# Merging the last column group of the up projections: two matmuls for three per weight tile

## The chip, the cores and the metric

The kernel runs on one core of a Trainium2 chip. The metric is the device time of one execution in microseconds (us), as the median of several runs. TensorE is called PE here, VectorE DVE, ScalarE ACT, GpSimd POOL; L1979 is line 1979 of the kernel file.

## The reference

Two blocks of two layers each work on x with 256 tokens and 1024 features, in float32. Six feed-forward networks (FFNs) lie on the path, one after the other: two in the first block, four in the second. In short:

```python
def conv_ffn(h, w_up, conv_w, conv_b, w_down):        # FFN 0 and 1
    gu = h @ w_up                                     # 1024 -> 2 * 2816
    g, u = gu[..., :D_FF], gu[..., D_FF:]
    g = causal_depthwise_conv3(g, conv_w) + conv_b
    return (silu(g) * u) @ w_down                     # 2816 -> 1024

def swiglu(x, w13, w2):                               # FFN 2 to 5
    gate, up = jnp.split(x @ w13, 2, axis=-1)
    return (silu(gate) * up) @ w2
```

Between them stand a state-space mixer, a stick-breaking attention and, twice, a mixer of sliding-window attention and a gated delta rule. The change touches only the up projections `h @ w_up` and `x @ w13`.

## The kernel before

**Precision.** Each operand of a projection is split into a rounded part (hi) and its rest (lo), both in a rounded float32 format, and a product is made of three matmuls: hi*hi, hi*lo and lo*hi. Weights come from memory in panels of 512 rows by 512 columns (`plan`). A panel lands in `raw` (a ring of RAW = 2 slots), ACT rounds it into `w_hi` (L744, in `split_hi`), and DVE subtracts to get `w_lo` (L1239, in `split_lo`); `w_hi` and `w_lo` have SPL = 3 slots. PE waits for `lo_ready` before a panel, and frees the slot with `panel_used`. SP issues the load of panel p once `w_lo` of panel p - 2 is made.

**The up projection.** It has 11 column groups j = 0 to 10. Each group has 256 gate columns and 256 up columns, in four tiles of 128, and two panels (k tiles 0 to 3 and 4 to 7). There are two ways to compute a group:

- `features` (L1983): for each column tile and k tile the three matmuls of `product` (L1979 to L1981), each 256 tokens wide, with the sums of a group in one accumulator `acc` (1024 columns, four tiles of 256).
- `merged` (L2132): the activation's hi and rest lie side by side in `xT`, so one matmul 512 wide (L2148) multiplies `w_hi` with both and a second one 256 wide (L2149) adds `w_lo` times hi. The sums take twice the room, two accumulators of 1024 columns: half 0 for the two gate tiles, half 1 for the two up tiles.

Groups in `MERGED` (1 to 9) take the second way, groups 0 and 10 the first. Group 0 is worked through in the order in which its input arrives (L1995, L2002).

**Accumulators.** There are two, `acc[0]` and `acc[1]`, handed out in turn by a running number u (`up_uses`, L377, and `uses`): use u takes `acc[u % 2]`, and `claim(u)` (L1970) makes PE wait until use u - 2 is freed. A merged group with an even j takes two uses, u and u + 1; a merged group with an odd j takes none and lies in the two `turn_banks` (named trp in the rows). A plain group takes one use. The down projection that follows (`tokens`, L2029) takes two uses, one for each half of its 1024 columns: it has 6 panels for each half, 24 matmuls of 512 columns in a full one.

**Folding a merged group.** The hi and lo sums have to be added. In `ffn` of ACT, L783 copies the lo sums of half 0 and then of half 1 into `folds`. In `ffn` of DVE, L1375 adds half 0 (the gate), L1377 adds half 1 (the up part). For an even j, half 1 is freed by L1377 itself, half 0 by an increment of DVE's sequencer behind it, once L1375 is done. Then follow, for FFN 0 and 1, the convolution's bias tap on ACT (L790) and its two other taps on DVE (L1390, L1391), silu (L794, or L796 for FFN 2 to 5), the product with the up part (L1394), rounding into `hT_hi` (L803) and its rest `hT_lo` (L1404). A plain group goes straight from `acc` into L790 or L796.

**Order on ACT and DVE.** It is written out by `gemm`: for group j, the split of panel p0 + 3 (p0 is the first of the group's two panels), then the evacuation of group j (fold, taps, product), then the split of panel p0 + 4, then `hidden` (L803 or L1404). So for group 10 the split ahead of its evacuation is that of the second panel of the down projection. Both engines work their instructions off in this order.

The down projection waits for `hT_lo` of each pair of k tiles (`hlo_ready`); its last panel needs that of group 10.

Of the kernel before, what the change touches and what calls it, by code (L numbers as in the profile page):

```python
# [49 lines left out]
RAW, SPL = 2, 3  # L50
TRP = 4

MERGED = range(1, 10)

TWO_PI = 2 * math.pi
MAGIC = 1.5 * 2 ** 23
# [127 lines left out]
def build(nc, T, out):  # L184
# [4 lines left out]
    with es:  # L189
# [5 lines left out]
        def sem(name):  # L195
            if name not in sems:
                sems[name] = es.enter_context(nc.semaphore(name))
            return sems[name]
# [178 lines left out]
        def up_uses(name):  # L377
# [3 lines left out]
            for j, ps in enumerate(gemms[name]):  # L381
                pairs_at[name, j] = None if j in MERGED and j % 2 else n_use
                if pairs_at[name, j] is None:
                    turns.append((name, j))
                    continue
                for _ in range(2 if j in MERGED else 1):
                    filled[n_use] = (panel_used, ps[-1] + 1)
# [131 lines left out]
        def up_tiles(f, j):  # L519

            if j in MERGED:
                v = folds[:, j % 2]
            else:
                v = A4(place(f"up{f}", j))
            return v[:, 0:2], v[:, 2:4]

        def folded_no(f, j):
            return f * len(MERGED) + j - MERGED.start + 1

# [193 lines left out]
        def _(act):  # L723
# [50 lines left out]
            def ffn(f):  # L774
                def gate(j, u):
# [3 lines left out]
                    h, (g, _) = hbuf[:, hn % 2], up_tiles(f, j)  # L779
                    if j in MERGED:  # L780
                        act.wait_ge(panel_used, gemms[f"up{f}"][j][-1] + 1)
# [16 lines left out]
                def hidden(j, u):  # L798
                    if j in MERGED:
                        act.wait_ge(sem("fold_gated"), folded_no(f, j))  # L800
                    else:
                        wait_evacuated(act, u)
                    A(hT_hi[:, 2 * j:2 * j + 2, :], hbuf[:, (f * 11 + j) % 2], ACT.Copy).then_inc(sem("hhi_ready"), 1)  # L803
# [1915 lines left out]
```

## Time and profile before

| | |
|---|---|
| Time, median of 3 runs | 2141.79 us (2140.05 to 2143.49) |
| Profiled execution, its own time | 2142.33 us |
| Its span | 2140.5 us |
| PE busy with matmuls | 2075.5 us, 97% |
| PE weight loads | 1802.6 us, 84% |
| DVE, ACT, POOL busy | 1436.9 us (67%), 1060.7 us (50%), 159.5 us (7%) |
| Matmuls | 14848, each with one weight load |

The span is the time from the first to the last instruction; 1.8 us of the execution's time lie around it. A matmul's own duration is modelled and overlaps the next one's, so the pace of PE is read from the starts of its matmuls.

### The profile page before, as it was taken

How to read it: one execution, taken by the hardware profiler on the slowest of the kernel's cores; microseconds unless marked ns; L12 is line 12 of the kernel's file. 1: busy time of each engine (PE TensorE's matmuls, PEld its weight loads, DVE VectorE, ACT ScalarE, POOL GpSimd, SP SyncE). 2: the span in 40 equal slices, each digit the busy share in tenths (PEclk: the TensorE clock that was granted, in tenths of full speed). 3: DMA queues.
4: the chain of work that ended last, by engine and by line, in shares of the span. 5: the costliest groups of instructions: out<-in, count | busy, mean ns of one | idle time of the engine just before them, and what ended most of it. 6: DMA issues, size and time to landing. Idle time of an engine off the chain costs nothing.

```text
span 2140.5 us, 34287 instructions
## 1 busy us (share of the span) xinstructions
PE 2075.5 (97%) x14848; PEld 1802.6 (84%) x14848; DVE 1436.9 (67%) x1658; ACT 1060.7 (50%) x1266; POOL 159.5 (7%) x119
## 2 busy tenths in 40 slices
PE   7799999999999999999999999999999999999998
PEld 6788888988888888898778888888889977788886
DVE  8966765567765664775766776476558576677654
ACT  5545554655643553455544455345434564444542
POOL 1000000000001000440000010020005200002000
PEclk9799999999999999999999999999999999999999
DMA  7245655435555665554312475556546633135653
GB/s 153 71 156 163 197 187 167 158 118 177 178 188 186 197 197 177 176 198 138 120 41 100 154 216 182 184 184 204 186 154 203 203 119 118 42 118 171 203 187 128
DMA packets 259789, 342.45 MB, mean 160 GB/s; under 512 B 23383, under 2 KB 169469, under 8 KB 259639
## 3 DMA queue, kind: packets, MB, share of 16 engines
q1 hardware_dynamic: 254272, 329.95, 48.0%
q0 software_dynamic: 2768, 9.08, 1.4%
q10 hardware_dynamic: 2599, 1.23, 0.5%
q8 instruction: 117, 1.92, 0.4%
q14 instruction: 33, 0.27, 0.0%
HBM read 338.14 MB, written 2.10 MB: 159 GB/s over the span
## 4 chain that ended last, share of the span: by engine, by line
PE 85%; DVE 9%; DMA 1%; ACT 1%; issue 1%; POOL 0%; DVEq 0%; ACTq 0%
PE acc L1979 11%; PE acc L1981 11%; PE acc L1980 11%; PE trp L2148 10%; PE acc L2148 8%; PE trp L2149 5%; PE acc L2149 4%; PE acc L1995 3%; PE trp L1979 2%; PE trp L1981 2%; PE trp L1980 2%; DVE w_lo L1239 2%; PE acc L2002 1%; PE acc L2044 1%; DMA raw<-in_w_in 1%; PE acc L2561 1%
## 5 line engine op out<-in xcount | busy, mean ns | idle before, releaser
L1239 DVE TENSOR_TENSOR w_lo<-raw,w_hi 128x2048 fp32r<-128x2048 f32 x314 | 721.5, 2301 | 414.9 <-ACT w_hi L744 413.4
L744 ACT ACTIVATE w_hi<-raw 128x2048 fp32r<-128x2048 f32 x314 | 590.0, 1879 | 542.7 <-PE acc L1981 206.2
L2148 PE MATMUL trp<-xT,w_hi 128*128 128x512 f32 x960 | 338.5, 396 | 0.0
L2148 PE MATMUL acc<-xT,w_hi 128*128 128x512 f32 x768 | 270.8, 396 | 0.0
L2149 PE MATMUL trp<-xT,w_lo 128*128 128x256 f32 x960 | 269.4, 281 | 0.0
L2148 PEld LDWEIGHTS trp<-xT,w_hi 128*128 128x128 f32 x960 | 180.1, 188 | 43.0
L2149 PE MATMUL acc<-xT,w_lo 128*128 128x256 f32 x768 | 215.5, 281 | 0.0
L1981 PE MATMUL acc<-w_hi,hT_lo 128*128 128x512 f32 x528 | 209.3, 396 | 0.0
L1979 PE MATMUL acc<-w_hi,hT_hi 128*128 128x512 f32 x528 | 209.3, 396 | 0.0
L1980 PE MATMUL acc<-w_lo,hT_hi 128*128 128x512 f32 x528 | 209.3, 396 | 0.0
L1979 PE MATMUL acc<-xT,w_hi 128*128 128x256 f32 x704 | 201.3, 286 | 6.1 <-DVE w_lo L1239 6.1
L1980 PE MATMUL acc<-xT,w_hi 128*128 128x256 f32 x704 | 200.6, 285 | 0.0
L1981 PE MATMUL acc<-xT,w_lo 128*128 128x256 f32 x704 | 200.6, 285 | 0.0
L2149 PEld LDWEIGHTS trp<-xT,w_lo 128*128 128x128 f32 x960 | 181.4, 189 | 0.0
L2148 PEld LDWEIGHTS acc<-xT,w_hi 128*128 128x128 f32 x768 | 144.1, 188 | 34.6
L2149 PEld LDWEIGHTS acc<-xT,w_lo 128*128 128x128 f32 x768 | 145.1, 189 | 0.0
L1979 PEld LDWEIGHTS acc<-xT,w_hi 128*128 128x128 f32 x704 | 136.4, 194 | 7.4 <-issue 7.1
L1980 PEld LDWEIGHTS acc<-xT,w_hi 128*128 128x128 f32 x704 | 136.5, 194 | 0.1
L1981 PEld LDWEIGHTS acc<-xT,w_lo 128*128 128x128 f32 x704 | 136.5, 194 | 0.0
L1981 PEld LDWEIGHTS acc<-w_hi,hT_lo 128*128 128x128 f32 x528 | 99.5, 188 | 24.2
L1980 PEld LDWEIGHTS acc<-w_lo,hT_hi 128*128 128x128 f32 x528 | 99.5, 188 | 24.0
L1979 PEld LDWEIGHTS acc<-w_hi,hT_hi 128*128 128x128 f32 x528 | 99.5, 188 | 24.0
(438 smaller groups left out, 3438.7 us busy)
## 6 DMA issues: line engine op xcount, KB each, us to landing
raw<-in_ffn_w SPq DMA_DIRECT2D x184, 512.0 KB
raw<-in_w_in SPq DMA_DIRECT2D x60, 1024.0 KB
raw<-in_ffn_w_up SPq DMA_DIRECT2D x88, 512.0 KB
raw<-in_ffn_w SPq DMA_DIRECT2D x40, 1024.0 KB
raw<-in_ffn_w_down SPq DMA_DIRECT2D x20, 1024.0 KB
raw<-in_ssm_w_glu SPq DMA_DIRECT2D x16, 512.0 KB
raw<-in_kv_w SPq DMA_DIRECT2D x8, 1024.0 KB
raw<-in_w_branch_a SPq DMA_DIRECT2D x8, 1024.0 KB
```

The source lines that it names most:

```text
L744: A(w_hi[:, p % SPL, 0:kt, :], raw[:, p % RAW, 0:kt, :], ACT.Copy).then_inc(hi_ready, 1)
L1239: V_.tensor_tensor(w_lo[:, p % SPL, 0:kt, :], raw[:, p % RAW, 0:kt, :], w_hi[:, p % SPL, 0:kt, :].bitcast(F32), ALU.subtract).then_inc(lo_ ...
L1979: mm(out, ah, bh, start=first, stop=False, skip_group_check=True)
L1980: mm(out, ah, bl, start=False, stop=False, skip_group_check=True)
L1981: return mm(out, al, bh, start=False, stop=last, skip_group_check=True)
L1995: mm(out[:, n], w[:, p % SPL, k, n * P:n * P + P], src[0][:, k0 + k, :], start=i == k == 0 and w is w_hi and n % 2 == 0, stop=False, skip_ ...
L2002: ins = mm(out[:, n], w_hi[:, p % SPL, kk, n * P:n * P + P], src[1][:, k0 + kk, :], start=False, stop=i == len(gemms[name][j]) - 1 and kk ...
L2044: mm(out[:, t], src[0][:, k0 + k, t * P:t * P + P], w[:, p % SPL, k, :], start=i == k == 0 and w is w_hi, stop=False, skip_group_check=True)
L2148: mm(tile, w_hi[:, p % SPL, k, c], xT[:, k0 + k], start=i == k == 0, stop=False, skip_group_check=True)
L2149: ins = mm(tile[:, 0], w_lo[:, p % SPL, k, c], xT_hi[:, k0 + k, :], start=False, stop=i == len(gemms[name][j]) - 1 and k == kt - 1, skip_g ...
L2561: ins = mm(a[:, h * P:h * P + P], left[:, h, :], right[:, h, :], start=n == 0, stop=n == len(terms) - 1, skip_group_check=True)
```

## The change

Group 10 too is merged, in all six FFNs: its two panels are worked through with L2148 and L2149 in place of L1979 to L1981, and it goes through the folds. As it is even, it takes two accumulator uses where it took one, so all later uses have a number that is higher by one for each FFN passed. `folded_no` counts ten merged groups for each FFN where it counted nine.

```diff
-MERGED = range(1, 10)
+MERGED = range(1, 11)
```

## Rows read from the trace of the kernel before

**Rows 1.** The page: busy time of the engines; the chain that ended last, by engine.
```profile
PE 2075.5 (97%) x14848; PEld 1802.6 (84%) x14848; DVE 1436.9 (67%) x1658; ACT 1060.7 (50%) x1266; POOL 159.5 (7%) x119
...
PE 85%; DVE 9%; DMA 1%; ACT 1%; issue 1%; POOL 0%; DVEq 0%; ACTq 0%
```

**Rows 2.** Waits of PE: who waited for whom: us in total, times, longest us.
```profile
PE trp L2287 <- DVEq L1573: 6.2, 1, 6.2
PE acc L1979 <- DVE w_lo L1239: 6.1, 4, 2.3
```

**Rows 3.** Timeline of PE, FFN 0 and 1: start us, duration, engine, line, operation.
```profile
282.04 0.35 PE L1979 MATMUL acc<-xT,w_hi 128*128 128x256 f32 x1
...
293.63 0.39 PE L1979 MATMUL acc<-w_hi,hT_hi 128*128 128x512 f32 x1
...
607.63 0.39 PE L1979 MATMUL acc<-w_hi,hT_hi 128*128 128x512 f32 x1
```

**Rows 4.** Timeline of PE, FFN 2 and 4: first matmuls of group 9, group 10, down.
```profile
776.06 0.40 PE L2148 MATMUL trp<-xT,w_hi 128*128 128x512 f32 x1
...
787.37 0.28 PE L1979 MATMUL acc<-xT,w_hi 128*128 128x256 f32 x1
...
798.89 0.39 PE L1979 MATMUL acc<-w_hi,hT_hi 128*128 128x512 f32 x1
...
1508.28 0.39 PE L2148 MATMUL trp<-xT,w_hi 128*128 128x512 f32 x1
...
1519.37 0.28 PE L1979 MATMUL acc<-xT,w_hi 128*128 128x256 f32 x1
...
1530.88 0.39 PE L1979 MATMUL acc<-w_hi,hT_hi 128*128 128x512 f32 x1
```

**Rows 5.** Timelines of ACT and of DVE, FFN 2: the folds of group 9.
```profile
787.63 1.09 ACT L783 ACTIVATE folds<-trp 128x512 f32<-128x512 f32 x2 [3.73 <-PE trp L2149]
...
788.26 0.69 DVE L1375 TENSOR_TENSOR folds<-folds,trp 128x512 f32<-128x512 f32 x1 [2.03 <-ACT folds L783]
```

**Rows 6.** Timeline of DVE, FFN 0 and 1: what stands ahead of group 10's evacuation.
```profile
293.75 2.28 DVE L1239 TENSOR_TENSOR w_lo<-raw,w_hi 128x2048 fp32r<-128x2048 f32 x1
295.95 0.47 DVE L1390 SCALAR_TENSOR_TENSOR hbuf<-acc,cols,hbuf 128x255 f32<-128x255 f32 x1
...
300.36 2.29 DVE L1239 TENSOR_TENSOR w_lo<-raw,w_hi 128x2048 fp32r<-128x2048 f32 x1 [1.12 <-ACT w_hi L744]
...
607.13 2.29 DVE L1239 TENSOR_TENSOR w_lo<-raw,w_hi 128x2048 fp32r<-128x2048 f32 x1
609.34 0.48 DVE L1390 SCALAR_TENSOR_TENSOR hbuf<-acc,cols,hbuf 128x255 f32<-128x255 f32 x1
```

**Rows 7.** Timelines of DVE and of PE, near 22 us: one hand-over.
```profile
20.51 2.23 DVE L1239 TENSOR_TENSOR w_lo<-raw,w_hi 128x2048 fp32r<-128x2048 f32 x1
...
22.79 0.39 PE L1995 MATMUL acc<-xT,w_hi 128*128 128x256 f32 x1 [1.09 <-DVE w_lo L1239]
```

**Rows 8.** Timeline of PE: the longest waits behind 124 us, in brackets the idle us.
```profile
903.42 0.36 PE L1979 MATMUL acc<-xT,w_hi 128*128 128x256 f32 x1 [2.27 <-DVE w_lo L1239]
...
1095.05 0.27 PE L2566 MATMUL acc<-cst,U 64*64 64x64 f32 x1 [1.39 <-DVE U L1837]
...
1635.14 0.39 PE L1979 MATMUL acc<-xT,w_hi 128*128 128x256 f32 x1 [1.91 <-DVE w_lo L1239]
```

**Rows 9.** Windows: us, engines' busy time (instructions), PEclk, DMA share, GB/s.
```profile
905.00:910.00 5.00, 5.00 (x31) 5.00 (x31) 4.93 (x11) 1.44 (x2) 2.32 (x2) 0.67 0.97 363
910.00:915.00 5.00, 5.00 (x44) 5.00 (x43) 4.82 (x5) 3.29 (x3) 3.18 (x2) 1.00 0.34 84
...
1635.00:1640.00 5.00, 4.86 (x28) 4.89 (x29) 4.59 (x7) 1.79 (x5) 3.96 (x3) 0.66 0.75 243
...
1098.00:1103.00 5.00, 5.00 (x78) 4.14 (x77) 1.77 (x2) 4.97 (x4) 0.00 (x0) 1.00 0.00 0
```

**Rows 10.** Timeline of PE: third and sixth panel of the down projection, FFN 0.
```profile
304.88 0.40 PE L1979 MATMUL acc<-w_hi,hT_hi 128*128 128x512 f32 x1
...
321.74 0.40 PE L1979 MATMUL acc<-w_hi,hT_hi 128*128 128x512 f32 x1
```

**Rows 11.** Timeline of PE: two matmuls, 33 apart, in the v projection.
```profile
413.32 0.39 PE L1980 MATMUL acc<-w_lo,xT 128*128 128x512 f32 x1
...
420.80 0.39 PE L1980 MATMUL acc<-w_lo,xT 128*128 128x512 f32 x1
```

## The prediction

> **What bounds the kernel now.** I read the page's busy shares and the chain first, then PE's waits, then the timelines of PE, DVE and ACT around the end of an up projection. The reader is to see three things. PE is busy 97% of the span and holds 85% of the chain [rows 1]: what shortens or holds up its stream moves the end nearly one for one. Its waits are few and none of them lies at an up projection's end: the largest groups are 6.2 us at 101 us, and four waits for w_lo, 6.1 us together [rows 2]. And at an end the down projection's first matmul follows at the pace of the stream, 293.63 in FFN 0 and 798.89 in FFN 2 [rows 3, 4]: the accumulator that it claims has been free for long, because it is half 1 of group 8, folded while group 9 ran.
>
> **What the change removes: a third of group 10's weight loads.** Plain, group 10 takes 293.63 - 282.04 = 11.59 us in FFN 0, 798.89 - 787.37 = 11.52 in FFN 2 and 1530.88 - 1519.37 = 11.51 in FFN 4 [rows 3, 4]. That is 96 matmuls at 0.120. A merged group has 32 pairs. Group 9 in FFN 2 takes 787.37 - 776.06 = 11.31 us, 0.353 for a pair; in FFN 4 it takes 1519.37 - 1508.28 = 11.09, 0.347 for a pair [rows 4]. So the gain is small, 0.2 us in FFN 0 to 3, whose merged groups run nearly all at the first pace, and 0.4 in FFN 4 and 5 at the second: the columns that stream, 768 for each weight tile, are the same in both ways. If nothing else changed, the sum would be 4 x 0.2 + 2 x 0.4 = 1.6 us less.
>
> The Trainium skill, TensorE: Matmul & The Clock Gate, section "Wait — 56ns, not 53.3ns?", has a matmul cost its columns and some 2.5 ns more at full clock. By that, an estimate, one matmul fewer in each of 32 triples saves 0.08 us in a group and 0.5 us in all six. The trace speaks for more: a triple takes 360 ns and a pair 353 or 347. The stream's sum would be 0.5 less by the page and 1.6 less by the rows; the total below would rise by 1.1.
>
> **What it adds: PE waits for the fold at every up projection's end.** Group 10 now takes uses u and u + 1, and the first half of the down projection takes u + 2, which is the accumulator of group 10's half 0. Its claim waits until use u is freed, and that happens only when L783 has copied the lo sums and L1375 has added them. Behind the claim stands everything that PE has: 132 matmuls of that half, and then the rest of the program. No other claim is hit: group 10 claims what group 8 held, which was folded during group 9, and the down projection's second half claims group 10's half 1 some 30 us later. The change of parity everywhere behind leaves the order of claims as it is.
>
> The length of the wait, FFN 2 to 5. Here DVE is idle when the fold comes. Group 9 shows the chain: PE's next slot is at 787.37, ACT copies from 787.63, and L1375 runs from 788.26 to 788.95 [rows 4, 5]. That is 1.58 us behind the slot. Then DVE's sequencer sees its own semaphore, increments another, and PE starts. One such hand-over took 22.79 - (20.51 + 2.23) = 0.05 us [rows 7]; the trace shows none by way of a sequencer, so its bounds are 0.05 and twice to four times this, and I take two, 0.1. The down projection starts 1.68 us behind the slot. The split of panel p0 + 3 is ready before: it needs only group 10's first panel done. Against today, with the gain set off: in FFN 2 and 3 the slot is at 787.37 + 11.31 = 798.68, the start at 800.36 and not 798.89, +1.47 each. In FFN 4 and 5 the slot is at 1519.37 + 11.09 = 1530.46, the start at 1532.14 and not 1530.88, +1.26 each. Four of them make 2 x 1.47 + 2 x 1.26 = 5.5.
>
> FFN 0 and 1. Here DVE is late, since the taps of group 9 delay it: ahead of group 10's evacuation stands the w_lo split, from 293.75 to 296.03, and the next instruction starts at 295.95 [rows 6]. The fold add stands at that place, whatever PE does, and ACT's copies (from some 293.6, 0.55 each) are done by then. It takes 0.69 as in [rows 5], so half 0 is folded at 296.64 and PE starts at 296.74, not at 293.63: +3.1. In FFN 1 the same place is at 609.34 [rows 6], which gives 610.13 against 607.63: +2.5. In these two the group's own gain is swallowed by the wait. Together 5.6.
>
> **What it adds on ACT and DVE.** Two copies (1.09), two adds (1.37) for each FFN. They delay the split of the third down panel: today 300.36 to 302.65 in FFN 0 [rows 6], then about 2 us later, by 304.7. PE needs it at 304.88 today [rows 10] and, having waited, at 308.0. It is covered; if the wait were not there, 0.2 us would be all that is left of that cover. hT_lo of group 10 is due before the sixth panel, at 321.74 + 3.1, some 20 us after it is made. Nothing for either.
>
> **The clock.** The two longest waits behind 124 us idled PE 2.27 and 1.91 us. Right behind them the mean clock of five us is 0.67 and 0.66, and PE starts about 31 matmuls where it starts 44 at full clock [rows 8, 9]: 13 x 0.12 = 1.5 us are lost as part of the stretch runs at 1.2 in place of 2.4 GHz. Behind a wait of 1.39 us the clock stayed at 1.00 [rows 8, 9]. The new waits in FFN 0 and 1 idle PE for some 3.4 and 2.7 us, beyond both rows that fell, so I take 1.5 us for each: 3.0. Those in FFN 2 to 5 idle it for 1.7, between the row that held and the one that fell; I take nothing, and the bound is 4 x 1.5 = 6.0.
>
> **The sum.** 5.5 + 5.6 + 3.0 = 14.1 us more than the profiled execution's 2142.33, so 2156.4. The runs' median is 0.5 below that execution: 2155.9, say 2156.
>
> **The rivals.** (a) *The clock falls at all six ends.* For it: 1.7 is nearer to 1.91 than to 1.39. Against: a wait and a fall have only two cases in the trace. 2156 + 6 = 2162. (b) *The clock does not fall.* 2156 - 3 = 2153. (c) *The wait is hidden*: the first down matmuls find their accumulator free, as today, and what is left is the lighter stream. It needs half 0 freed within a matmul of group 10's end; if the fold took no longer than the 0.2 to 0.4 us that a group gains, it would break even. For it speaks that no group before this one was ever seen to wait. Against: the fold of [rows 5], with both engines idle before it, takes 1.58 us, and group 10 has no group behind it that lies elsewhere. 2141.8 - 1.6 = 2140, not slower. (d) *PE's pace changes behind the new waits.* Streams of 512 columns have two paces: 72 matmuls of the down projection take 321.74 - 304.88 = 16.86, 0.234 each, while in the v projection it is (420.80 - 413.32) / 33 = 0.227 [rows 10, 11]. If the wait put all six down projections (264 matmuls each) on the faster pace, 6 x 264 x 0.0074 = 11.7 us come back: 2156 - 11.7 = 2144. Against it: the down projection runs at 0.234 in all six FFNs, whichever pace its merged groups had, so it looks like a property of its operands. The smaller case, merged groups changing between 11.31 and 11.09 in one FFN, is worth 2 us either way.
>
> **How the numbers follow.** Forecast (clock down at FFN 0 and 1, here and there once more or less) 0.62, (a) 0.12, (b) 0.13, (c) 0.04, (d) 0.05, and 0.04 for something not seen. The time is that of the likeliest, 2156. The range reaches from (b) with the merged groups' faster pace in two FFNs, 2149, to (a) and a little more, 2163; it leaves out (c), (d) and the tail. A measurement of this kernel can tell about 0.2%, 4.3 us, from no change: slower than 2146.1 is 0.90, from (d) 0.05 and (c) 0.03 within it 0.08, faster 0.02.
>
> **What would show it.** PE's waits should list the first down matmul six times, behind DVE's fold (L1375, or the sequencer behind it), 1.6 to 1.8 us in FFN 2 to 5 and 2.5 to 3.4 in FFN 0 and 1, some 13 us together. The stretches after those in FFN 0 and 1 should have a clock below 1.00 for a part of 5 us. Group 10 should take 11.3 or 11.1 us, and PE's instruction count fall by 192, to 14656. The forecast is wrong if the down projection starts within 0.5 us of group 10's end, if the clock stays up behind 3 us, or if another stretch gives the time back: the four waits for w_lo of [rows 2] come 60 us and more behind an up projection's end, and their loads are issued relative to PE's own progress, so I expect none of it there.

## The result, and the profile after

| | before | after |
|---|---|---|
| Median of 6 runs each | 2139.2 us (2134.1 to 2143.5) | 2149.8 us (2148.4 to 2152.4) |
| Ratio to before | | 1.0056, 95% interval 1.0046 to 1.0066 |
| Profiled execution, its time; span | 2142.33; 2140.5 us | 2149.43; 2147.5 us |
| PE busy | 2075.5 us | 2070.1 us |
| Matmuls | 14848 | 14656 |

The change makes the kernel slower by 0.56%, 12.0 us (9.8 to 14.1). The ratio is not the quotient of the two medians, which are 10.6 us apart; both lie inside the interval. PE's matmuls fell by 192, as they should, its busy time by 5.4 us, and yet the end came later. The page after, first line of its busy times and the chain by engine, against [rows 1]:

```profile
PE 2070.1 (96%) x14656; PEld 1784.4 (83%) x14656; DVE 1447.3 (67%) x1670; ACT 1067.9 (50%) x1278; POOL 151.8 (7%) x119
...
PE 74%; DVE 16%; ACT 4%; DMA 2%; issue 2%; POOL 0%; DVEq 0%; SPq 0%; ACTq 0%
```

PE's share of the chain fell from 85% to 74%, and DVE's rose from 9% to 16%. The six new waits alone don't do that: a kernel further down ("fold first") has all six, and its page still says PE 85% and DVE 9%. The shift comes from FFN 0 and 1. There the fold came late because DVE was late, and from that point the chain leads back through DVE and ACT along nearly the whole up projection: `w_hi`, `w_lo`, `hT_lo`, `w_lo`, fold, taps, silu and the next `w_hi`. In FFN 2 to 5 it leaves PE only for the fold at the end. One turn of that loop in FFN 0 takes 11.35 us, here from one w_lo split of DVE to the next, where a merged group takes PE 11.31:

```profile
278.60 2.29 DVE L1239 TENSOR_TENSOR w_lo<-raw,w_hi 128x2048 fp32r<-128x2048 f32 x1 [1.11 <-ACT w_hi L744]
...
289.95 2.29 DVE L1239 TENSOR_TENSOR w_lo<-raw,w_hi 128x2048 fp32r<-128x2048 f32 x1 [1.11 <-ACT w_hi L744]
```

So in FFN 0 and 1 these two engines together are as near to being the limit as PE. PE's waits after (who waited for whom: us in total, times, longest us), against [rows 2], name the new one:

```profile
PE acc L1979 <- DVEq L1384: 10.9, 6, 2.9
...
PE acc L1979 <- DVE w_lo L1239: 4.0, 4, 1.4
```

L1384 is the increment by DVE's sequencer that frees the first half of group 10's accumulators. PE never waited for it before; now it does, once in each FFN. PE's timeline after, at the end of the up projection in FFN 0, 1 and 2 (start us, duration, and in brackets the idle us and who ended it), against [rows 3] and [rows 4]:

```profile
292.60 0.28 PE L2149 MATMUL acc<-xT,w_lo 128*128 128x256 f32 x1
295.76 0.79 PE L1979 MATMUL acc<-w_hi,hT_hi 128*128 128x512 f32 x1 [2.87 <-DVEq L1384]
...
610.98 0.28 PE L2149 MATMUL acc<-xT,w_lo 128*128 128x256 f32 x1
613.17 0.50 PE L1979 MATMUL acc<-w_hi,hT_hi 128*128 128x512 f32 x1 [1.91 <-DVEq L1384]
...
804.21 0.28 PE L2149 MATMUL acc<-xT,w_lo 128*128 128x256 f32 x1
806.01 0.51 PE L1979 MATMUL acc<-w_hi,hT_hi 128*128 128x512 f32 x1 [1.52 <-DVEq L1384]
```

The two other engines' timelines after, ACT and then DVE, show what the waits are made of. In FFN 2 both were idle: PE's last matmul starts at 804.21, ACT copies from 804.59, DVE adds from 805.22 to 805.91, and PE starts 0.10 later. In FFN 0 ACT's copies start at 292.98, but DVE is in w_lo until 295.04, and the add starts at 294.96:

```profile
292.98 1.08 ACT L783 ACTIVATE folds<-acc 128x512 f32<-128x512 f32 x2 [0.73 <-PE acc L2149]
...
804.59 1.09 ACT L783 ACTIVATE folds<-acc 128x512 f32<-128x512 f32 x2 [3.74 <-PE acc L2149]
```
```profile
292.76 2.28 DVE L1239 TENSOR_TENSOR w_lo<-raw,w_hi 128x2048 fp32r<-128x2048 f32 x1
294.96 0.68 DVE L1375 TENSOR_TENSOR folds<-folds,acc 128x512 f32<-128x512 f32 x1
...
805.22 0.69 DVE L1375 TENSOR_TENSOR folds<-folds,acc 128x512 f32<-128x512 f32 x1 [2.05 <-ACT folds L783]
```

**By stage.** From PE's starts, for each FFN the time from the first matmul of group 1 to the first of the down projection ("up"), and from there to the down projection's last ("down"):

| FFN | up before | up after | down before | down after |
|---|---|---|---|---|
| 0 | 113.42 | 116.11 | 61.61 | 63.16 |
| 1 | 113.28 | 115.14 | 61.61 | 61.72 |
| 2 | 113.28 | 114.76 | 61.61 | 61.72 |
| 3 | 113.27 | 112.72 | 61.61 | 61.72 |
| 4 | 111.47 | 114.76 | 61.61 | 61.73 |
| 5 | 111.46 | 114.76 | 61.61 | 61.72 |

FFN 1 and 2 ran their merged groups at the same pace in both profiles and show the change alone: +1.86 and +1.48. (FFN 0 did so but for its last two groups before, 11.32 and 11.35.) FFN 3, 4 and 5 also changed between the two paces of a merged group, 11.3 and 11.1 us, which nine or ten groups make 2 us. The down projection is 0.11 longer everywhere, as its first matmul behind a wait takes 0.11 more to the next, and 1.55 longer in FFN 0, where the clock fell.

### The profile page after: what moved, and what is told of

Read it like the earlier page. It is cut to its first block, busy times and chain, and to the rows that moved or that the text cites. A ratio compares the mean times of both kernels' runs of the same rounds, so it can differ in the third digit from the quotient of the medians.

```text
span 2147.5 us, 33939 instructions
## 1 busy us (share of the span) xinstructions
PE 2070.1 (96%) x14656; PEld 1784.4 (83%) x14656; DVE 1447.3 (67%) x1670; ACT 1067.9 (50%) x1278; POOL 151.8 (7%) x119
## 4 chain that ended last, share of the span: by engine, by line
PE 74%; DVE 16%; ACT 4%; DMA 2%; issue 2%; POOL 0%; DVEq 0%; SPq 0%; ACTq 0%
PE acc L1979 10%; PE acc L1981 10%; PE acc L1980 10%; PE trp L2148 7%; PE acc L2148 7%; DVE w_lo L1239 6%; PE trp L2149 4%; PE acc L2149 4%; PE acc L1995 3%; PE trp L1979 2%; ACT w_hi L744 2%; PE trp L1981 2%; PE trp L1980 2%; PE acc L2044 1%; DMA raw<-in_w_in 1%
## 5 line engine op out<-in xcount | busy, mean ns | idle before, releaser
L2148 PE MATMUL trp<-xT,w_hi 128*128 128x512 f32 x960 | 339.7, 398 | 0.0
L2148 PE MATMUL acc<-xT,w_hi 128*128 128x512 f32 x960 | 339.5, 398 | 0.0
L2149 PE MATMUL trp<-xT,w_lo 128*128 128x256 f32 x960 | 269.1, 280 | 0.0
L2149 PE MATMUL acc<-xT,w_lo 128*128 128x256 f32 x960 | 269.0, 280 | 0.0
L1979 PE MATMUL acc<-w_hi,hT_hi 128*128 128x512 f32 x528 | 210.7, 399 | 10.9 <-DVEq L1384 10.9
L2148 PEld LDWEIGHTS acc<-xT,w_hi 128*128 128x128 f32 x960 | 180.3, 188 | 44.5
L2148 PEld LDWEIGHTS trp<-xT,w_hi 128*128 128x128 f32 x960 | 180.4, 188 | 44.2
L1981 PE MATMUL acc<-w_hi,hT_lo 128*128 128x512 f32 x528 | 209.8, 397 | 0.0
L2149 PEld LDWEIGHTS trp<-xT,w_lo 128*128 128x128 f32 x960 | 181.2, 189 | 0.0
L2149 PEld LDWEIGHTS acc<-xT,w_lo 128*128 128x128 f32 x960 | 181.1, 189 | 0.0
L1979 PE MATMUL acc<-xT,w_hi 128*128 128x256 f32 x512 | 145.6, 284 | 4.0 <-DVE w_lo L1239 4.0
L1980 PE MATMUL acc<-xT,w_hi 128*128 128x256 f32 x512 | 144.9, 283 | 0.0
L1981 PE MATMUL acc<-xT,w_lo 128*128 128x256 f32 x512 | 144.9, 283 | 0.0
L1979 PEld LDWEIGHTS acc<-w_hi,hT_hi 128*128 128x128 f32 x528 | 99.8, 189 | 36.9 <-DVEq L1384 12.8
L1981 PEld LDWEIGHTS acc<-w_hi,hT_lo 128*128 128x128 f32 x528 | 99.8, 189 | 24.4
L658 POOL TENSOR_TENSOR nrm<-nrm 128x1 f32<-128x1 f32 x22 | 13.6, 617 | 1390.1 <-DVE nrm L1274 832.1
L1979 PE MATMUL trp<-w_hi,xT 128*128 128x512 f32 x256 | 104.7, 409 | 0.0
L1979 PEld LDWEIGHTS acc<-xT,w_hi 128*128 128x128 f32 x512 | 98.2, 192 | 4.7 <-issue 4.7
```

The costliest lines, as they stand in the source:

```text
L658: tt(nrm[:, 3, one], nrm[:, 0, one], nrm[:, 1, one], ALU.pow).then_inc(sem("root_ready"), 1)
L1979: mm(out, ah, bh, start=first, stop=False, skip_group_check=True)
L1980: mm(out, ah, bl, start=False, stop=False, skip_group_check=True)
L1981: return mm(out, al, bh, start=False, stop=last, skip_group_check=True)
L2148: mm(tile, w_hi[:, p % SPL, k, c], xT[:, k0 + k], start=i == k == 0, stop=False, skip_group_check=True)
L2149: ins = mm(tile[:, 0], w_lo[:, p % SPL, k, c], xT_hi[:, k0 + k, :], start=False, stop=i == len(gemms[name][j]) - 1 and k == kt - 1, skip_g ...
```

## The experiments

The table has all runs; each ratio is to the kernel before, run on the same chip in the same rounds. Differences in us below are worked out from the ratios.

| Kernel | Median us | Before, same rounds | Ratio, 95% interval |
|---|---|---|---|
| group 10 merged, down in turn bank | 2137.95 | 2138.95 | 0.9997 (0.9988 to 1.0006) |
| group 10 plain, wait added | 2159.3 | 2138.95 | 1.0092 (1.0079 to 1.0106) |
| merged, fold first | 2150.02 | 2138.95 | 1.0045 (1.0032 to 1.0057) |
| the changed kernel again | 2151.75 | 2138.95 | 1.0057 (1.0043 to 1.0071) |
| group 10 plain, down in turn bank | 2136.55 | 2136.36 | 1.0000 (0.9991 to 1.0010) |
| merged, down in turn bank, again | 2137.41 | 2136.36 | 1.0003 (0.9992 to 1.0013) |
| the kernel before, again, one execution | 2141.55 | 2136.36 | |

**The merge without the wait.** The first half of the down projection gets the turn bank that group 9 left. It takes one accumulator use less for each FFN, so its second half claims group 10's half 0 and later uses have lower numbers; nothing else of the changed kernel differs. The main lines of the edit; `...` stands for lines left out, which call `down_uses` and give this use a semaphore of its own for being freed:

```diff
+        def down_uses(f):
...
+            name = f"down{f}"
+            pairs_at[name, 0], pairs_at[name, 1] = -1 - f, n_use
...
         def A2(u):
+            if u < 0:
+                return turn_banks[0][:, :].rearrange("p (t n) -> p t n", t=2)
...
             def claim(u):
 
+                if u < 0:
+                    pe.wait_ge(sem("turn_freed"), turns.index((f"up{-1 - u}", 9)) + 1)
+                    return
```

> Group 10 is merged as in the changed kernel, but the first half of the down projection sums in turn bank 0, which group 9 left a whole group earlier, so its claim waits for nothing new. If the wait for the fold of group 10 is the cost (my theory): the six waits (10.9 us) and the clock's fall behind FFN 0 (1.5 us) go, and the time is 12 us below the changed kernel and within 2 us of the kernel before (some 2138). If the merged matmuls or the added folds themselves cost (rival): it stays within 4 us of the changed kernel, 2146 to 2154.

The ratio is 0.9997, and the whole loss is gone: 12.8 us between this kernel's ratio and that of the changed kernel in the same rounds (0.0060 x 2139). The rival, that the merged matmuls or the folds themselves cost, falls: this kernel has both. In PE's timeline of this kernel the down projection (L1998 here) follows the last merged matmul of FFN 2 at the stream's own pace, 0.12 behind it, and the line of the waits for DVE's sequencer is gone:

```profile
797.45 0.28 PE L2168 MATMUL acc<-xT,w_lo 128*128 128x256 f32 x1
797.57 0.40 PE L1998 MATMUL trp<-w_hi,hT_hi 128*128 128x512 f32 x1
```

From group 1 to the down projection FFN 1 to 5 take 113.07 us each, where the kernel before took 113.28 at the same pace of merged groups. So 0.21 us is what the merge saves in an FFN at the slower pace.

**The wait without the merge.** One line in the kernel before:

```diff
+                wait_evacuated(pe, place(f"up{f}", 10))
                 for j in range(2):
                     tokens(f"down{f}", j, use[f"down{f}"] + j, hT,
```

> The kernel before, group 10 plain, but PE waits before the down projection until group 10's accumulator is freed. That is when L1394 has run: in FFN 2 to 5 1.6 us behind the group (798.89 to 800.5), in FFN 0 5.6 us (293.63 to 299.3), in FFN 1 5.0 us. If a wait at this place is paid one for one (my theory): 4 x 1.6 + 5.6 + 5.0 = 17 us, and 1.5 us of clock in FFN 0 and in FFN 1: 20 us above the kernel before, some 2159. If a wait there is given back later, by loads that then lie ahead (rival; in the changed kernel the two mixer stretches were 6.7 us shorter than before): 10 us or less, below 2150.

It came to 2159.3, ratio 1.0092, 19.7 us (16.9 to 22.7), against 20 expected. PE's waits, and its first down matmuls in FFN 0 and FFN 2:

```profile
PE acc L1979 <- DVE hbuf L1394: 16.1, 6, 5.5
```
```profile
299.82 0.80 PE L1979 MATMUL acc<-w_hi,hT_hi 128*128 128x512 f32 x1 [5.50 <-DVE hbuf L1394]
...
816.00 0.50 PE L1979 MATMUL acc<-w_hi,hT_hi 128*128 128x512 f32 x1 [1.47 <-DVE hbuf L1394]
```

16.1 us of waits and 4.4 us of lower clock (the down projections of FFN 0 and 1 took 63.88 and 63.75 instead of 61.61) make 20.5. The rival, 10 us or less, falls: a wait at this place is paid nearly in full. That nothing at all of it comes back isn't shown, as the interval leaves room for some 3 us. A fall of the clock cost more here than the 1.5 us expected, 2.2 and 2.0 us over a down projection's 61.72 behind a wait: the granted clock was 0.50 through all of 298 to 304 us, where the changed kernel's was back at 1.00 at 300.

**Fold first.** For group 10, DVE's w_lo split of the next panel goes behind the two adds (`...` stands for lines left out, among them `gate`'s new argument):

```diff
-                    for p in ps[:-1]:
-                        if p <= last - hold:
+                    ahead = [p for p in ps[:-1] if p <= last - hold]
+                    first = name.startswith("up") and j == 10
+                    if not first:
+                        for p in ahead:
                             split_lo(p + SPL)
-                    evacuate(j, place(name, j))
+                    evacuate(j, place(name, j), *([lambda: [split_lo(p + SPL) for p in ahead]] if first else []))
...
                             wait_evacuated(dve, u + 1)
+                        if then:
+                            then()
```

> The changed kernel, but for group 10 DVE folds first and makes the w_lo of the second down panel behind the folds. If in FFN 0 and 1 the fold was late because it stood behind that w_lo (my theory): the wait of FFN 0 falls from 2.9 to about 1.6 us and that of FFN 1 from 1.9 to 1.6, and the clock holds behind FFN 0: 1.7 to 3.3 us less than the changed kernel, 2147. Rival: ACT's copies or the taps of group 9 are what is late, and moving w_lo gains nothing (within 0.5 us in the two waits).

The profile shows the expected order at work: in FFN 0 DVE now adds at 293.40, as soon as the first copy is made, and PE waits 1.52 us, as in FFN 2; FFN 1 shows 1.52 too. DVE's timeline, then PE's (L1377 and L1983 here are L1375 and L1979 of the changed kernel), then PE's waits:

```profile
293.40 0.69 DVE L1377 TENSOR_TENSOR folds<-folds,acc 128x512 f32<-128x512 f32 x1 [0.92 <-ACT folds L783]
294.01 0.68 DVE L1379 TENSOR_TENSOR folds<-folds,acc 128x512 f32<-128x512 f32 x1
294.72 2.29 DVE L1239 TENSOR_TENSOR w_lo<-raw,w_hi 128x2048 fp32r<-128x2048 f32 x1
```
```profile
294.20 0.50 PE L1983 MATMUL acc<-w_hi,hT_hi 128*128 128x512 f32 x1 [1.52 <-DVEq L1386]
```
```profile
PE acc L1983 <- DVEq L1386: 9.2, 6, 1.5
```

The clock held behind all six waits. Six times 1.5 us is left. DVE already adds as soon as the first copy is made, so no other order on DVE can shorten that part; copying and adding in smaller pieces wasn't tried. The ratio went from 1.0057 to 1.0045, 2.6 us by the middle values; the two intervals overlap, so the gain in time fits the 1.7 to 3.3 us expected but isn't shown by the times alone. The place of the fold also moves the chain: PE 85% and DVE 9% again, with all six waits still there.

**The changed kernel again, for the pace and the clock.** No edit.

> The changed kernel as it is, profiled once more. In its first profile the merged groups took 11.3 us each in FFN 0, 1, 2, 4 and 5 and 11.1 in FFN 3; in the kernel before they took 11.3 in FFN 0 to 3 and 11.1 in FFN 4 and 5. If the pace belongs to the execution (my theory): another set of FFNs is at 11.1 here, with the same six waits (within 0.1 us each). If it belongs to the program (rival): again only FFN 3.

This time FFN 5 alone ran its merged groups at 11.1 us (112.73 from group 1 to down) and the other five at 11.3. So the pace belongs to the execution. The waits were the same but for DVE's place in FFN 0: 10.6 us in six. And the clock fell twice, behind FFN 0 and FFN 1, where the first profile has one fall, behind FFN 0. Windows (us, busy time of PE, its weight loads, DVE, ACT, POOL with instructions, then the granted clock), the first two of the first profile of the changed kernel, the other two of the second:

```profile
295.60:298.90 3.30, 3.14 (x7) 2.48 (x8) 2.49 (x6) 1.17 (x3) 0.00 (x0) 0.50 1.05 364
...
611.00:616.00 5.00, 3.09 (x14) 2.32 (x13) 4.29 (x7) 2.18 (x4) 0.00 (x0) 1.00 0.95 331
```
```profile
296.40:299.60 3.20, 3.20 (x9) 2.53 (x8) 1.91 (x5) 1.15 (x4) 0.00 (x0) 0.50 1.03 378
613.90:617.10 3.20, 3.20 (x9) 2.50 (x8) 1.95 (x5) 1.15 (x3) 0.00 (x0) 0.50 1.03 379
```

A clock of 0.50 is 1.2 GHz. The wait of FFN 1 was 1.9 us long in both profiles (2190 and 2189 ns from start to start), and the clock held behind it in one and fell in the other. Each fall costs 1.4 to 1.5 us: 63.16 or 63.25 for a down projection in place of 61.72.

**The same accumulators, group 10 plain.** The down projection's first half in the turn bank, but `MERGED = range(1, 10)`:

> The kernel before, group 10 plain, with the first half of the down projection in turn bank 0: set beside the same with group 10 merged, it leaves the merge alone. If the merge saves what the pace of its stream says (my theory), group 10 takes 11.5 us here and 11.3 there, 1.3 us over six, and this kernel's time is that of the kernel before within 1 us. If taking turn bank 0 itself costs or saves (rival), it differs from before by more than 2 us.

> Group 10 merged and the first half of the down projection in turn bank 0, timed again: 1.3 us below the plain one with the same accumulators if only the stream counts, level with it or above if the two more copies and adds for each FFN reach the path.

1.0000 and 1.0003: taking the turn bank costs nothing that these rounds can tell, and the saving of the merge is too small for them too. A kernel that is 1.3 us faster, 0.9994, would lie inside both intervals, and the middle value has the other sign. In the profiles the saving is there: 113.28 against 113.07 us in an FFN at the slower pace, and 111.46 against 111.05 at the quicker.

**The kernel before again.**

> The kernel before, profiled once more. In its first profile the two mixer stretches (from the down projection of FFN 2 and of FFN 4 to the next up projection) took 367.7 and 367.4 us, in the changed kernel's 364.1 and 364.3. If that is spread of executions (my theory): 364 to 366 here. If the change made them shorter (rival): again 367.4 to 367.7.

A miss, in part: the two stretches took 367.95 and 364.61 us. The second agrees with spread of executions; the first does not, as all three profiles with group 10 plain and nothing added have 366.5 to 368.0 there, and all five with it merged have 364.1 to 364.8. It doesn't take the wait at the down projection: one of the five is the merged kernel without it (364.55). The kernel with the wait alone lies between, 365.4. The waits for w_lo at the start of the mixer's input projections are 6.1, 6.1 and 6.2 us in the three plain kernels' profiles and 3.6 to 4.3 in the five merged ones. The longest one, 2.3 to 2.4 us in the plain kernels, was followed by a fall of the clock; the longest of the merged ones, 1.3 to 1.8 us, was not. Nor was the wait of 1.75 us in the short stretch of this profile, the one of 364.61. PE reaches that point at the same distance from the down projection's end (40.4 us) with group 10 plain (the kernel before, twice) and merged (in the turn bank). The load that it waits for landed 9.64 us behind its release in the kernel before and 8.76 in the changed one. Why is open. The medians give no sign of it: both kernels with the turn bank, plain and merged, took the same time, while their profiled executions took 2142.1 (plain) and 2138.9 and 2135.7 (merged). So it may belong to profiled executions only; that wasn't tried.

## Why the prediction was right

- **The stream's gain.** 0.2 us in an FFN at the slower pace and 0.4 at the quicker were forecast, and 0.21 and 0.41 measured (113.28 to 113.07, 111.46 to 111.05). Weighing it by which FFNs are at which pace was idle, as the pace changes from one execution to the next. By the Trainium skill (TensorE: Matmul & The Clock Gate, "Wait — 56ns, not 53.3ns?") it would have been 0.08, an estimate; the measurement decides for the rows.
- **The claim.** Right in place and mechanism: six waits, released by the increment behind L1375.
- **FFN 2 to 5.** 1.68 us behind the slot were forecast. The slot is 0.12 behind the start of the last matmul, so in FFN 2 it is 804.33 and the start 806.01: 1.68. Net +1.48 measured for +1.47, and at the quicker pace +1.26 for +1.26 (112.72 in FFN 3 after, 111.46 in FFN 5 before). The hand-over through the sequencer took the 0.10 assumed.
- **FFN 0 and 1.** The fold did stand behind w_lo, which the fold-first kernel shows. The size was somewhat high, +2.7 and +1.9 for +3.1 and +2.5: DVE's w_lo started 0.4 and 0.6 us sooner, measured from group 1, than in the profile of before (113.11 for 113.54 us, 112.15 for 112.78). The difference isn't a drift over the up projection: DVE's fold of group 2 already came that much sooner (24.51 for 24.94, 23.55 for 24.19), and from there on DVE and ACT go at their own 11.35 us a group in both. So "the taps of group 9 delay it" was only the last part of the cause. What sets the size is when the loop gets going at the start of the up projection, and the 0.04 us by which each turn is slower than PE. The second profile of the changed kernel has 112.81 in FFN 0, that of the kernel before 113.22, so one profile bounds the wait there to some 0.3 us. Where in FFN 1 the 0.4 to 0.7 us between the kernels with group 10 plain (112.55 to 112.86) and merged (112.15 to 112.17, the fold-first one aside) come from is open.
- **The clock.** 1.5 us for a fall was right (1.44 and 1.53). Two falls were forecast; one profile has one and the other two. None came behind a new wait of 1.5 us, of which the two profiles, that of fold first and that of the wait alone hold eighteen, so rival (a) is out. To take nothing for these four was a choice between a row that held at 1.39 and one that fell at 1.91; it came true, and the rows had not settled it.
- **The sum.** Local terms of the changed kernel at equal pace: 2.7 + 1.9 + 4 x 1.48 = 10.5 for the waits less the gain, 6 x 0.11 = 0.7 for the first matmuls, which I had left out, and 1.5 to 3.1 for the clock: 12.7 to 14.3. Measured by the ratios: 12.0 and 12.2, so the local sum is itself somewhat high, inside the intervals. Forecast: 14.1. Against the local sum, FFN 0 and 1 were put 1.0 us too high, and in one profile the second fall 1.5; the first matmuls, left out, were 0.7 too low, and part of the error cancels.
- **The level.** The median of before was 2139.2 over all its runs instead of 2141.8 over the three that were shown, and the medians lie 10.6 us apart where 14.1 was forecast: 2.6 and 3.5 us put 2149.8 some 6 us below the 2156 forecast. By the ratio the difference was off by only 2. The profiled execution of the kernel before is at the upper end of its own runs, and I took my base there. 2149.8 is 0.8 us above the range's lower end, which rival (b) had set for a clock that never falls; that it still lies inside is in part luck.
- **What was not foreseen.** The difference of the two profiles alone, 7.1 us, is smaller than that of the medians, as the two mixer stretches were 6.7 us shorter after. That is the prediction's own sign of being wrong, another stretch that gives the time back, and at the waits for w_lo where none was expected. Read alone it would have passed for that. But these stretches are nearly as short in the merged kernel that has no wait (729.9 and 730.1 us for the two together; 728.4 in the changed kernel, 735.1 before), and the kernel with the wait alone, 730.4 in its profile, still pays nearly all of its waits by the ratio. Why all of these are shorter than the plain kernels' stays open.

The version with the turn bank is as fast as the kernel before, not measurably faster: with its wait gone, what is left of the merge is 0.2 to 0.4 us in each of six FFNs.

## What to carry to other kernels

Before a step takes a second buffer of a small ring, write down who claims each buffer next and how long behind the step's end it is freed. Here a saving of 0.2 us in matmuls bought a wait of 1.7 us, since the stage behind had lived on the buffer that the step now takes. Count streamed columns before counting matmuls: three matmuls of 256 columns and two of 512 and 256 stream the same. Look at the pace of the engines that feed PE too: in FFN 0 and 1 DVE and ACT took 11.35 us a group and PE 11.31, so a fold placed behind their work came late. And when one profile differs from another in stages that the change doesn't touch, profile both again before explaining it.

## What the runs showed of the hardware

- The merged pairs have two paces, 347 and 353 ns, which last for whole up projections (but for the first group at the quicker one, 11.2 us) and change between executions of one program: FFN 4 and 5 fast, then FFN 5 alone, for the kernel before; FFN 3, then FFN 5, for the changed one. All nine or ten groups together are 1.8 to 2.0 us in an FFN, more than the merge saves. At full clock, the plain groups (0.120 for each matmul) and the down projection (0.234) showed one pace only, the latter behind a wait of 1.5 to 5.5 us too.
- PE's idle time does not tell alone whether the clock falls. Behind waits of 1.47 to 1.53 us at the up projections' ends it never fell (eighteen cases); of 1.9 us, it fell in one execution and not in another of the same program; of 2.6 us and more, always. At the mixers' input projections it held behind six of 1.41 to 1.84 us and fell behind 1.87 and 1.91 and behind all three of 2.3 to 2.4. In the delta rule's stage of small matmuls one fall came behind a gap of 1.85 us from start to start; in another execution of the same program the same gap had none, nor had one of 2.12 us in the fold-first kernel.
- The clock was low for 3.4 us behind waits of 1.9 to 2.9 us, which lost 1.4 to 1.5 us, and for 6.8 us around those of 5.5 and 4.7 us, where it fell before the wait ended; 2.2 and 2.0 us were lost behind them.
- The first matmul of 512 columns behind a wait took 0.11 us more to the next one than the others, at full clock (0.34 for 0.234).
- From the end of DVE's add, by way of the increment of its sequencer, to PE's start it took 0.10 to 0.12 us.
